# Two fused transformer blocks: the front and the indexer in another order, modulations moved into the gates, merging products moved into the last attention head

## The chip, the core and the metric

The kernel runs on one core of a Trainium2 chip. The metric is the device time of one execution in microseconds (us). Five engines work side by side, each through its own queue of instructions: PE (TensorE, matmuls; PEld are its weight loads), DVE (VectorE), ACT (ScalarE), POOL (GpSimd) and SP (SyncE, which here only starts transfers). They wait for each other through semaphores. Transfers between the main memory and the on-chip memory are done by 16 DMA engines, and are started here from the queues of SP, POOL and ACT. PSUM is the memory with eight banks into which PE writes.

## The reference

The input x has 1024 tokens of 1024 features. A first block and then two layers of a second block are applied to it. The change lies in the first block:

```python
h = rms_norm(x, g_mix)
aq, ak, av, bq, bk, bv, iq, ik, iw, cx, cy, gt = split_cols(h @ w_in)
y_a = chunk_relpos_attention(...)                       # 4 heads
q_i = apply_rope(iq, cos, sin); k_i = apply_rope(rms_norm(ik, g_idx_k), cos, sin)
# indexer: 4 heads of 64; each query keeps the 256 keys with the largest score
dots  = einsum('bqhe,bse->bqhs', q_i, k_i)
score = einsum('bqhs,bqh->bqs', relu(dots), w_i)
y_b = attention over the kept keys                      # 4 heads
y_c = rglru_branch(cx, cy, ...)                         # a linear recurrence (LRU)
gates  = sigmoid(gt + b_gate)                           # 3 x 1024 features
merged = gates[0] * (y_a @ wb_a) + gates[1] * (y_b @ wb_b) + gates[2] * (y_c @ wb_c)
x = x + merged @ w_out                                  # then a feed-forward part
```

Each layer of the second block scales and shifts its normed input by numbers that come from a condition alone, `silu(cond) @ w_ada + b_ada` (1024 x 3072 weights for each of two layers). These products are called modulations here: they need nothing of the first block and can be computed at any time before it ends. Its differential attention needs a number lambda, `exp(sum) - exp(sum) + const`, and sinks, which also depend on weights alone.

## The kernel before

All large products keep about single precision with three passes: each operand is split into a high part (a cast to a shorter format) and a low part (the rest), and `matmul3` (L2939) sums high x high, high x low and low x high. A split therefore takes an ACT cast (L3137 for weights, L3141 for values, L3154 for normed rows) and a DVE subtraction (L3297, L3300, L3322).

`schedule()` writes one list of steps in program order; then one function per engine goes through the list and issues its engine's share. So the order in which `schedule()` adds steps is the order on every engine's queue, and a step that waits holds up all later steps of its engine. The stages up to the merge are, in the profile's time:

- 0 to 79 us, the front. `t_x` loads x in 16 tiles (8 row groups, 2 chunks of 512 tokens) from POOL's queue, and `t_c` the constants from SP's. `w_load` and `w_prep` load and split weights (`w_get(name, ahead)` hands one out and prepares the next). `first_sums(c)` squares a chunk (ACT L3145 squares one tile, DVE L3305 squares and adds), `first_norm` then needs column sums on PE (L2976), the root on ACT (L3150), its reciprocal (DVE L3308), a spread over rows (PE L2983) and the scaling of every tile (DVE L3317). `cond` is the silu of the condition (ACT L3190). The three projections of the indexer are `ik`, `q0`, `q1` (weights ikw, iq0, iq1).
- up to 146 us, the keys and the indexer. `begin` rotates q or k (PE L2990, DVE L3330, POOL L3720), `end` sums the rotation (DVE L3334) and splits it. The keys stand on partitions 0 to 63 and are copied to 64 to 127 by DMA, since the four heads of the indexer use the two halves. `lambda` is on DVE (L3346), ACT (L3178) and DVE (L3349 to L3352). `index` is PE's product of a block b of 128 queries with its keys, one for each of four heads (24 in all, counted by `nr`); ACT takes the relu (L3183), DVE weighs and adds it (L3361, L3364).
- 146 to 473 us, eight column blocks (cx, cy) of the recurrent branch and 24 gates (`gt`), each 16 steps of three matmuls; a gate's result is stored from ACT's queue (L3132). DVE finds the largest scores here. Then the LRU.
- the attention heads, and from 931 us the merge: for each of 8 output groups d and 2 chunks c three places, `wb_first` (place 0, four steps of the recurrent branch), then the other two branches; DVE multiplies each by its gate (L3484 and following). In the last head the attention leaves PE time, into which a `Fill` of other steps is drawn (`early_steps` and the tail `wb_early`).

A modulation is eight small matmuls (PE L3021, 2 columns by 512), with two weight loads of 512 KB from SP's queue through a ring of buffers (`m_fetch`, L3748); after every second one `modrows` copies a row (ACT L3188), and the next modulation first does a turning (`m_turn`, PE L3026). There are 24 of them.

## Time and profile before

| | |
|---|---|
| median of 3 runs | 3783.07 us (3779.55 to 3783.47) |
| profiled execution | 3786.55 us, of which the span of the trace 3784.4 us |
| mean granted clock of PE | 0.952 |
| PE busy | 91% of the span |
| DVE, ACT, POOL busy | 56%, 37%, 8% |
| bytes moved | 257.16 MB |

A line number is that of the kernel before. In a row of the timeline the first number is the start after the span's beginning and the second the time the group takes; in brackets stands how long the engine had been idle and what it waited for. `m` is a buffer in on-chip memory, `PS` one in PSUM, `in_...` an input in main memory. A row with "x7" is a run of seven instructions. In the table of stretches the granted clock is a share of full speed: 1.00 stands for 2.4 GHz and 0.50 for 1.2 GHz.

### The profile page before, as it was taken

The numbers are of one execution on the slowest core, as the hardware profiler recorded it, in microseconds if no ns is written. First come the engines' busy times: TensorE is split into PE (matmuls) and PEld (weight loads), VectorE is DVE, ScalarE is ACT, GpSimd is POOL, SyncE is SP. The second block draws the span as 40 slices with busy tenths as digits, with TensorE's granted clock in tenths as the row PEclk, the third lists the DMA queues.
The fourth block names the chain that finished last, engine by engine and source line by source line (L and its number), as shares of the span: only waits on it lengthen the run. The fifth ranks groups of instructions, "written<-read, shape, count | busy, mean of one in ns | idle before, by whom it ended". The sixth has DMA issues, their size and how long they took to land. (4 is left out here: it accounts for less than half of the span.)

```text
span 3784.4 us, 43717 instructions
## 1 busy us (share of the span) xinstructions
PE 3455.7 (91%) x17694; PEld 2679.9 (71%) x17694; DVE 2124.7 (56%) x3918; ACT 1411.4 (37%) x2581; POOL 297.7 (8%) x431
## 2 busy tenths in 40 slices
PE   6999988897998999999899988888799999988888
PEld 4677766565877888887765677777677666676677
DVE  5799953444757666665556554455354444334444
ACT  3322264444233222322333244444324555434441
POOL 1122210001111000000000000000001000000000
PEclk9799999998999999999999998998799999989999
DMA  3333320002522222332210100010211101010112
GB/s 123 117 123 134 139 91 17 30 23 100 189 92 73 77 82 84 111 131 81 84 31 25 49 23 30 23 36 33 102 64 62 33 33 33 23 35 7 35 54 85
DMA packets 76632, 257.16 MB, mean 68 GB/s; under 512 B 9928, under 2 KB 11976, under 8 KB 76432
## 3 DMA queue, kind: packets, MB, share of 16 engines
q1 hardware_dynamic: 42192, 132.68, 10.5%
q0 software_dynamic: 30784, 109.12, 8.3%
q10 hardware_dynamic: 3456, 12.58, 0.8%
q8 instruction: 139, 2.28, 0.2%
q14 instruction: 61, 0.50, 0.0%
HBM read 193.53 MB, written 50.32 MB: 64 GB/s over the span
## 5 line engine op out<-in xcount | busy, mean ns | idle before, releaser
L2940 PE MATMUL PS<-m,m 128*128 128x512 f32 (+3 forms) x3476 | 1395.5, 403 | 84.2 <-DVE m L3297 16.8
L2942 PE MATMUL PS<-m,m 128*128 128x512 f32 (+3 forms) x3476 | 1338.3, 386 | 0.0
L2941 PE MATMUL PS<-m,m 128*128 128x512 f32 (+3 forms) x3476 | 1337.1, 386 | 0.0
L2940 PEld LDWEIGHTS PS<-m,m 128*128 128x128 f32 (+2 forms) x3476 | 664.3, 192 | 318.9 <-issue 77.0
L2942 PEld LDWEIGHTS PS<-m,m 128*128 128x128 f32 (+2 forms) x3476 | 664.1, 192 | 133.7 <-issue 0.8
L2941 PEld LDWEIGHTS PS<-m,m 128*128 128x128 f32 (+2 forms) x3476 | 667.7, 193 | 119.7 <-issue 1.5
L3229 ACT COPY m<-PS 128x512 f32<-128x512 f32 x352 | 205.1, 588 | 455.2 <-PE PS L3056 454.6
L3066 PE MATMUL PS<-m,m 128*64 128x256 f32 (+1 forms) x1408 | 307.8, 410 | 28.7 <-ACT m L3229 21.6
L3300 DVE TENSOR_TENSOR m<-m,m 128x512 fp32r<-128x512 f32 (+3 forms) x303 | 233.6, 790 | 163.0 <-ACT m L3141 161.9
L3141 ACT CAST m<-m 128x512 fp32r<-128x512 f32 (+3 forms) x303 | 198.7, 690 | 327.7 <-DVE m L3514 182.8
L3047 PE MATMUL PS<-m,m 64*128 64x256 f32 (+5 forms) x1968 | 248.0, 362 | 45.3 <-ACT m L3218 25.7
L3047 PEld LDWEIGHTS PS<-m,m 64*128 64x128 f32 (+1 forms) x1968 | 209.4, 193 | 93.8 <-ACT m L3218 33.6
L3056 PE MATMUL PS<-m,m 128*128 128x128 f32 x1408 | 227.7, 286 | 49.2 <-DVE m L3589 21.1
L3297 DVE TENSOR_TENSOR m<-m,m 128x1024 fp32r<-128x1024 f32 (+4 forms) x156 | 160.9, 1031 | 167.7 <-ACT m L3137 166.8
L3056 PEld LDWEIGHTS PS<-m,m 128*128 128x128 f32 x1408 | 169.7, 145 | 118.5 <-issue 39.8
L3161 ACT COPY m<-PS 128x512 f32<-128x512 f32 (+2 forms) x187 | 101.7, 549 | 331.9 <-PE PS L2942 331.8
L3066 PEld LDWEIGHTS PS<-m,m 128*64 128x64 f32 (+1 forms) x1408 | 155.0, 167 | 83.9 <-ACT m L3229 40.2
L3137 ACT CAST m<-m 128x1024 fp32r<-128x1024 f32 (+4 forms) x187 | 168.0, 900 | 120.0 <-PE PS L2942 58.0
L3520 DVE TENSOR_REDUCE m<-PS 128x1 f32<-128x1024 f32 x96 | 114.3, 1219 | 150.9 <-PE PS L3047 150.8
L3541 DVE CUSTOM_DVE_ANT_0 m<-PS,m 128x640 f32<-128x640 f32 (+7 forms) x128 | 93.1, 727 | 183.8 <-PE PS L3047 99.7
L3218 ACT ACTIVATE m<-PS,m 128x256 f32<-128x256 f32 (+1 forms) x272 | 188.1, 704 | 14.6 <-DVE m L3525 14.6
L3495 DVE TENSOR_TENSOR m<-m,PS 128x512 f32<-128x512 f32 x180 | 123.2, 685 | 116.5 <-PE PS L2942 113.6
(204 smaller groups left out, 3198.8 us busy)
## 6 DMA issues: line engine op xcount, KB each, us to landing
m<-in_w SPq DMA_DIRECT2D x222, 512.0 KB, 3.8
g_scratch<-m ACTq DMA_DIRECT2D x24, 512.0 KB, 2.6
m<-g_scratch POOLq DMA_DIRECT2D x24, 512.0 KB, 4.8
u_scratch<-m POOLq DMA_DIRECT2D x40, 256.0 KB, 3.2
m<-u_scratch POOLq DMA_DIRECT2D x20, 512.0 KB, 4.2
m<-in_w SPq DMA_DIRECT2D x40, 256.0 KB, 4.0
x_scratch<-m POOLq DMA_DIRECT2D x2, 4096.0 KB, 13.4
m<-m POOLq DMA_DIRECT2D x60, 128.0 KB, 2.7
```

Source lines behind the costliest of these rows:

```text
L2940: pe.e.engine.matmul(o, L[0], X[0], start=start, stop=False)
L2941: pe.e.engine.matmul(o, L[0], X[1], start=False, stop=False)
L2942: return pe.e.engine.matmul(o, L[1], X[0], start=False, stop=stop)
L3047: m = e.matmul(o, L, X, start=first, stop=last)
L3056: m = e.transpose(PS[:, s["out"] + 128 * i:s["out"] + 128 * i + 128], x, ident)
L3066: m = e.matmul(O, L, X, start=start, stop=stop)
L3137: e.copy(s["hi"], s["src"]).then_inc(*act.says(S.hi, ("w", s["i"])))
L3141: e.copy(s["hi"], s["src"]).then_inc(*act.says(S.hi, n))
L3218: m = e.activation(d, src if bias is None else d, ACT.Exp, bias=sums[:, 0:1], scale=scale, accum_out=sums[:, 3 + a:4 + a])
L3229: e.copy(s["h"], s["src"]).then_inc(*act.says(S.hi, ("pt", s["u"], s["g"])))
L3297: e.tensor_tensor(s["lo"], s["src"], s["hi"].bitcast(F), ALU.subtract).then_inc(*dve.says(S.lo, ("w", s["i"])))
L3300: e.tensor_tensor(s["lo"], s["src"], s["hi"].bitcast(F), ALU.subtract).then_inc(*dve.says(S.lo, n))
```

## The change

The first half's squares come before the weights' casts; the cast of the third weight and the silu come after the first norm; four of the x tiles are loaded from ACT's queue. The keys are summed, split and copied by chunks, and q0's and q1's second halves and lambda come between the indexer's blocks. The first three modulations leave the front, two leave the indexer, and every gate up to the last modulation runs one. In the last head the merging product of (output group 0, chunk 0) moves from the tail into the fill, and that of (1, 0) enters the tail.

```diff
@@ -1254,3 +1254,4 @@
     t_c = [move(vec[:, :], vec_d[:, 0:NVEC]), move(cst[:, :], cst_d)]
-    t_x = {(k, t0): move(X[:, k, t0:t0 + tn], xT[k][:, t0:t0 + tn]) for t0, tn in CH1 for k in range(8)}
+    t_x = {(k, t0): move(X[:, k, t0:t0 + tn], xT[k][:, t0:t0 + tn], on="pool" if t0 or k % 2 else "act")
+           for t0, tn in CH1 for k in range(8)}
     t_blam = move(blam[:, :], vec_d[:, NVEC:NVEC + 256])
@@ -1320,10 +1321,10 @@
 
+    early_sums = first_sums(0)
     w_prep(2)
-    p.add("cond", csil=csil[:, :], cond=vc("cond", 0, 16))
-    first = first_norm(0, first_sums(0))
+    first = first_norm(0, early_sums)
     next(first)
     w_load(3)
-    w_prep(3)
-    m_fetch(RING, [t_x[7, 0]])
     finish(first)
+    w_prep(3)
+    p.add("cond", csil=csil[:, :], cond=vc("cond", 0, 16))
 
@@ -1357,5 +1358,3 @@
             second = first_norm(1, late_sums)
-            steps_of(ik, 6)
-            modulate()
-            steps_of(ik, 2)
+            steps_of(ik, 8)
             steps_of(q0, 8)
@@ -1439,14 +1438,14 @@
             finish(q1)
-            modulate()
-            p.add("lambda", blam=[blam[:, 64 * i:64 * i + 64] for i in range(4)], ld=ld[:, :], lam=lam_t, after=t_blam,
-                  sink=vc("sink", 0, 8), nsink=nsink[:, :])
-            k_t = end("k", 0) + end("k", 1)
-            d1 = move(ikh[64:128, :], ikh[0:64, :], k_t)
-            d2 = move(ikl[64:128, :], ikl[0:64, :], k_t)
+            key_t = []
+
+            def keys_down(c):
+                t0, tn = CH1[c]
+                t = end("k", c)
+                key_t.append([move(x[64:128, t0:t0 + tn], x[0:64, t0:t0 + tn], t) for x in (ikh, ikl)])
+
+            keys_down(0)
             begin("q1", 1)
-            end("q0", 1)
-            modulate(last=True)
-            end("q1", 1)
+            keys_down(1)
             ring, m_rows = late_ring, late_rows
-            m_fetch(2 * m_next[0] + RING, normed + [(S.mod, m_all[m_next[0] - 1])])
+            m_fetch(RING, normed)
             b = take()
@@ -1456,3 +1455,2 @@
             bank_free[b] = [(S.score, "wi")]
-            p.add("ready", on="pe", after=qk_t + [d1, d2])
             r_free = [[], []]
@@ -1462,2 +1460,10 @@
                 sc = score[b]
+                if b in (2, 4):
+                    p.add("ready", on="pe", after=qk_t + key_t[b // 2 - 1])
+                if b == 2:
+                    end("q0", 1)
+                    p.add("lambda", blam=[blam[:, 64 * i:64 * i + 64] for i in range(4)], ld=ld[:, :], lam=lam_t, after=t_blam)
+                if b == 3:
+                    end("q1", 1)
+                    p.add("lambdas", lam=lam_t, sink=vc("sink", 0, 8), nsink=nsink[:, :])
                 for h in range(4):
@@ -1478,3 +1484,3 @@
                     nr += 1
-                    if nr % 4 == 0:
+                    if nr >= 12 and nr % 4 == 0:
                         modulate(nr == 24, [(S.lru, "lambda")])
@@ -1547,3 +1553,3 @@
                 for n, _ in enumerate(linear_steps(f"gt{i}_{d}", h_rhs, CH1, ev_s)):
-                    if n == 7 and n_g % 2 == 0 and m_next[0] < len(m_all):
+                    if n == 7 and m_next[0] < len(m_all):
                         modulate()
@@ -1626,7 +1632,8 @@
 
-            def wb_early():
-                y_held["w"] = w_get("wb0")
-                for c in range(2):
-                    b = y_held[c] = (7, 0)[c]
-                    yield from wb_first(0, c, b, y_held["w"])
+            def wb_early(jobs):
+                for d, c, b in jobs:
+                    if c == 0:
+                        y_held[d] = w_get(f"wb{d}", 2 - d)
+                    y_held[d, c] = b
+                    yield from wb_first(d, c, b, y_held[d])
             for kind in "ab":
@@ -1666,2 +1673,3 @@
                         yield from early_steps(list(ready) + list(second))
+                        yield from wb_early([(0, 0, 7)])
                     for k_, j_ in nxt:
@@ -1715,4 +1723,4 @@
                 more = (8 if nxt and nxt[0][0] == "b" else 6) + 32 if nxt else 0
-                at.run(units, ready, Fill(steps(), more + (18 if n_ab else 0) + (0 if nxt else 14)), 18 if n_ab else 0, tail,
-                       None if nxt else Fill(wb_early(), 8))
+                at.run(units, ready, Fill(steps(), more + (18 if n_ab else 0) + (0 if nxt else 18)), 18 if n_ab else 0, tail,
+                       None if nxt else Fill(wb_early([(0, 1, 0), (1, 0, 2)]), 8))
                 if nxt:
@@ -1737,10 +1745,10 @@
             y_ready[k] = split(Yh[:, k, :], Yl[:, k, :], y_in[:, k, 0:T], [y_there[k]])
-        p.turns += (1 - p.turns) % 6
+        p.turns += (4 - p.turns) % 6
         for d in range(8):
-            get, kt, release, event = weights = y_held["w"] if d == 0 else w_get(f"wb{d}")
+            get, kt, release, event = weights = y_held[d] if d in y_held else w_get(f"wb{d}")
             for c, (t0, tn) in enumerate(CH1):
                 for place, (i, k0, k1) in enumerate(((2, 4, 8), (0, 0, 2), (1, 2, 4))):
-                    b = y_held[c] if d == 0 and place == 0 else take()
+                    b = y_held[d, c] if place == 0 and (d, c) in y_held else take()
                     key = (f"wb{d}", c, i)
-                    if d and place == 0:
+                    if place == 0 and (d, c) not in y_held:
                         finish(wb_first(d, c, b, weights))
@@ -1762,2 +1770,4 @@
             release((S.lin, key))
+            if d == 0:
+                w_prep(st["use"] + 1)
         p.fence(False)
@@ -3347,2 +3357,4 @@
                                        lam[:, 2 + i:3 + i]).then_inc(*dve.says(S.lru, ("lambda", i)))
+        elif s.kind == "lambdas":
+            lam = s["lam"]
             dve.wait_ge(S.lruact, "lambda")
```

ACT's queue at the start of the program, before (m_67 is x, m_51 and m_52 raw weights, m_57 the vectors):

```order
L3137 ACT_TABLE_LOAD
L3137 CAST m_53<-m_51 128x544
L3137 CAST m_54<-m_52 128x1024
L3190 ACT_TABLE_LOAD
L3190 ACTIVATE m_65<-m_57 128x16
L3145 ACTIVATE m_70<-m_67 128x512
```

The squares (L3145, in the changed kernel L3155) are now the first work of the queue, behind four tile loads; the casts of the two weights follow them.

ACT's queue after the change, from the last scaled tiles of the first norm to the first squares of the second half (m_82 is the third weight's high part, m_65 the silu):

```order
L3164 CAST m_49<-m_71 128x512
L3164 CAST m_49<-m_72 128x512
L3147 CAST m_82<-m_51 128x1024
L3200 ACT_TABLE_LOAD
L3200 ACTIVATE m_65<-m_57 128x16
L3155 ACTIVATE m_76<-m_67 128x512
L3155 ACTIVATE m_74<-m_67 128x512
L3155 ACTIVATE m_75<-m_67 128x512
```

Before, the squares (L3145) stood directly behind the scaled tiles (L3154), and the cast of m_82 before them.

DVE's queue at the keys, before (m_97 is the keys, m_103 their low part, m_60 holds lambda):

```order
L3330 TENSOR_TENSOR m_105<-PS,m_59 128x512
L3346 ISA m_80,m_60<-m_81 128x64
L3346 ISA m_60 128x1
L3346 ISA m_80,m_60<-m_81 128x64
L3346 ISA m_60 128x1
L3349 TENSOR_TENSOR m_60<-m_60 128x1
L3351 TENSOR_SCALAR m_60<-m_60 128x1
L3352 TENSOR_SCALAR m_60<-m_57 128x8
L3334 TENSOR_TENSOR m_97<-m_108,m_109 64x512
L3300 TENSOR_TENSOR m_103<-m_97,m_102 64x512
```

The same queue after the change (m_95 is q0, m_114 the head weights wi):

```order
L3340 TENSOR_TENSOR m_105<-PS,m_59 128x512
L3344 TENSOR_TENSOR m_97<-m_108,m_109 64x512
L3310 TENSOR_TENSOR m_103<-m_97,m_102 64x512
L3340 TENSOR_TENSOR m_107<-PS,m_59 128x512
L3344 TENSOR_TENSOR m_97<-m_110,m_111 64x512
L3310 TENSOR_TENSOR m_103<-m_97,m_102 64x512
L3367 TENSOR_SCALAR m_114<-PS 128x32
L3344 TENSOR_TENSOR m_95<-m_104,m_105 128x512
L3310 TENSOR_TENSOR m_100<-m_95,m_98 128x512
L3356 ISA m_80,m_60<-m_81 128x64
```

The key sums have moved ahead of lambda, and lambda behind q0's second half.

PE's queue in the last head before, from the last products of attention with values to the last scores (m_49 and m_50 are the halves of two of the recurrent branch's groups, m_53 and m_55 those of the weight):

```order
L3066 MATMUL PS<-m_186,m_156 64x256 x2
L3047 MATMUL PS<-m_154,m_152 128x512 x2
L3047 MATMUL PS<-m_155,m_152 128x512 x2
L3047 MATMUL PS<-m_154,m_153 128x512 x2
L3047 MATMUL PS<-m_154,m_152 128x512 x2
L3047 MATMUL PS<-m_155,m_152 128x512 x2
L3047 MATMUL PS<-m_154,m_153 128x512 x2
L2940 MATMUL PS<-m_49,m_53 128x512
L2941 MATMUL PS<-m_50,m_53 128x512
L2942 MATMUL PS<-m_49,m_55 128x512
```

After the change, behind the last scores (m_190 and m_191, m_150 and m_151 are two more groups of the recurrent branch):

```order
L3057 MATMUL PS<-m_154,m_153 128x512 x2
L2950 MATMUL PS<-m_49,m_53 128x512
L2951 MATMUL PS<-m_50,m_53 128x512
L2952 MATMUL PS<-m_49,m_55 128x512
L2950 MATMUL PS<-m_190,m_53 128x512
L2951 MATMUL PS<-m_191,m_53 128x512
L2952 MATMUL PS<-m_190,m_55 128x512
L2950 MATMUL PS<-m_150,m_53 128x512
L2951 MATMUL PS<-m_151,m_53 128x512
L2952 MATMUL PS<-m_150,m_55 128x512
L2950 MATMUL PS<-m_49,m_53 128x512
L2951 MATMUL PS<-m_50,m_53 128x512
```

Where one step of a merging product stood behind the scores, four stand now: three of the moved product (its first stands ahead of the scores) and the first of the tail.

## Rows read from the trace of the kernel before

**Rows 1.** busy time by engine and its share of the span, from the page
```profile
PE 3455.7 (91%) x17694; PEld 2679.9 (71%) x17694; DVE 2124.7 (56%) x3918; ACT 1411.4 (37%) x2581; POOL 297.7 (8%) x431
```

**Rows 2.** five stretches: us, busy time by engine, granted clock, DMA share
```profile
core 0: us, PE busy (x) PEld busy (x) DVE busy (x) ACT busy (x) POOL busy (x), PEclk, DMA share, GB/s
2.00:9.00 7.00, 0.00 (x0) 0.00 (x0) 0.28 (x1) 0.46 (x1) 6.55 (x13) 1.00 0.96 326
79.00:86.00 7.00, 6.94 (x10) 2.75 (x11) 3.30 (x6) 0.00 (x0) 3.74 (x3) 0.51 0.01 2
93.00:137.00 44.00, 35.10 (x153) 23.01 (x155) 18.74 (x30) 14.26 (x23) 2.39 (x3) 0.50 0.42 130
146.00:473.00 327.00, 327.00 (x1513) 260.00 (x1512) 325.88 (x609) 69.41 (x91) 66.19 (x32) 1.00 0.34 127
931.00:1024.00 93.00, 92.82 (x393) 74.42 (x393) 75.97 (x106) 18.32 (x26) 9.04 (x18) 0.98 0.45 157
```

**Rows 3.** timeline of the front, all engines: start, length, what ended the wait
```profile
8.54 1.28 ACT L3137 ACT_TABLE_LOAD   x1 [8.54 <-DMA m<-in_cst]
...
9.84 1.59 ACT L3137 CAST m<-m 128x544 fp32r<-128x544 f32 x2
...
12.74 0.21 ACT L3190 ACTIVATE m<-m 128x16 f32<-128x16 f32 x1
...
21.68 1.03 ACT L3137 CAST m<-m 128x1024 fp32r<-128x1024 f32 x1
...
33.28 0.62 ACT L3154 CAST m<-m 128x512 fp32r<-128x512 f32 x1 [0.64 <-DVE m L3317]
...
34.98 5.47 DVE L3305 TENSOR_TENSOR m<-m,m 128x512 f32<-128x512 f32 x7 [0.36 <-ACT m L3145]
...
41.34 0.95 PE L2976 MATMUL PS<-m,m 128*128 128x1 f32 x8
```

**Rows 4.** timeline from 76 to 110 us, the keys
```profile
79.06 5.63 PE L2990 MATMUL PS<-m,m 64*64 64x512 f32 x6 [2.62 <-DVE m L3312]
...
88.16 0.58 ACT L3161 COPY m<-PS 128x512 f32<-128x512 f32 x1 [10.52 <-PE PS L2942]
...
91.62 0.68 DVE L3334 TENSOR_TENSOR m<-m,m 64x512 f32<-64x512 f32 x1
...
96.22 1.10 POOL L3708 DMA_DIRECT2D m<-m  x2 [10.17 <-DVE m L3300]
...
104.73 0.69 PE L2940 MATMUL PS<-m,m 64*128 64x384 f32 x2 [7.90 <-DMA m<-m]
```

**Rows 5.** DMA issues from 84 to 150 us: KB each, us to landing
```profile
m<-m POOLq DMA_DIRECT2D x2, 256.0 KB, 7.6
```

**Rows 6.** DMA issues of the whole span, from the page
```profile
m<-in_w SPq DMA_DIRECT2D x222, 512.0 KB, 3.8
...
m<-m POOLq DMA_DIRECT2D x60, 128.0 KB, 2.7
```

**Rows 7.** timeline of PE in the indexer, up to cx0
```profile
113.58 1.87 PE L3026 MATMUL PS<-m,m 128*128 128x2 f32 x8
115.38 1.89 PE L3021 MATMUL PS<-m,m 128*2 128x512 f32 x8
...
124.20 0.79 PE L2940 MATMUL PS<-m,m 64*128 64x512 f32 x1
...
145.66 0.50 PE L2940 MATMUL PS<-m,m 128*128 128x512 f32 x1
```

**Rows 8.** timeline of ACT in the gates, the stores alone
```profile
263.16 0.33 ACTq L3132 DMA_DIRECT2D g_scratch<-m  x1
...
276.05 0.33 ACTq L3132 DMA_DIRECT2D g_scratch<-m  x1
...
286.93 0.33 ACTq L3132 DMA_DIRECT2D g_scratch<-m  x1
...
299.00 0.33 ACTq L3132 DMA_DIRECT2D g_scratch<-m  x1
```

**Rows 9.** timeline of DVE, the first LRU step
```profile
489.27 1.23 DVE L3434 TENSOR_TENSOR m<-m,m 128x1024 f32<-128x1024 f32 x1 [12.65 <-ACT m L3203]
```

More of the change, by code:

```diff
@@ L1319, in first_sums @@
         return sums
+    early_sums = first_sums(0)
     w_prep(2)
-    p.add("cond", csil=csil[:, :], cond=vc("cond", 0, 16))
-    first = first_norm(0, first_sums(0))
+    first = first_norm(0, early_sums)
     next(first)
     w_load(3)
+    finish(first)
     w_prep(3)
-    m_fetch(RING, [t_x[7, 0]])
-    finish(first)
+    p.add("cond", csil=csil[:, :], cond=vc("cond", 0, 16))
     with mem:
```

## The prediction

> **What bounds the kernel now.** The first view to read is the busy time by engine [rows 1]: PE (TensorE) is busy 91% of the span, so a change that shortens the kernel must take work or waiting out of PE. The second is the table by stretch [rows 2], which says where there is something to take: from 146 to 473 us (the column blocks of the recurrent branch and the gates) PE is busy all 327.00 us at a granted clock of 1.00, so there every instruction more is paid in full; from 93 to 137 us (end of the front, the indexer) it is busy only 35.10 of 44 us, at a clock of 0.50, that is at 1.2 GHz instead of 2.4; from 931 to 1024 us (the merge) it is again full, 92.82 of 93 us. The third view is the timeline of the places that the change edits: the front [rows 3], the keys [rows 4, 5, 6], the indexer [rows 7], the gates [rows 8] and the first LRU step [rows 9]. The reader is to see in rows 4 that the indexer's first product starts at 104.73 after 7.90 us of waiting for a copy by DMA, and that behind the wait stands a chain: the lambda exponential, the key sum on DVE at 91.62, the POOL issues at 96.22, and the landing 7.6 us later [rows 5].
>
> **Front.** In what follows f is how much later the second half's norm ends. On ACT the two casts (1.59), the table load (1.28, the length of the one at 8.54) and the silu (0.21) leave the place ahead of the first squares [rows 3]: 3.08 us in all, less the 0.1 by which such instructions overlap, 3.0, and that is what the first half gains, g, if the constants still land at 8.54. They may not: the DMA engines are 0.96 busy at 326 GB/s from 2 to 9 us [rows 2], and four x tiles of 256 KB now set out on ACT's queue instead of behind the others on POOL's; 1.05 MB at 326 GB/s is 3.2 us, so the constants land 0 to 3.2 us later. I take the middle, g = 1.45, since no row shows which queue goes first. In the second half the cost turns round. Before, the late squares followed the last norm cast (33.28 + 0.62) at once; now the cast of the third weight (1.03, which stood at 21.68), a table load (1.28) and the silu (0.21) lie between: 2.5 us on the path, as DVE's additions wait for ACT's squares there. The additions end at 34.98 + 5.47 = 40.45 before; now at 34.98 + 2.5 + 0.1 − g + 5.47, some 43.0 − g. PE's column sums stood at 41.34, held by PE's own products in front of them; those now end at 41.3 − g, so PE waits 1.7 to 1.95 us and f = 1.7 − g = +0.25 (−1.3 to +1.7). A wait of that size also touches the clock: the 2.62 us of idleness at 79.06 [rows 4] was followed by 7 us at 0.51 [rows 2], which costs 7 × 0.49 = 3.4. Whether this shorter wait does the same no row says; between 0 and 3.4 I take 1.7. So f = 1.9 us in the forecast, −1.3 to +5.1 at the ends.
>
> The four moved tiles meet a rule of the Trainium skill, in "DMA: Bandwidth & Descriptors", section "Issuing engines are not separate DMA queues": transfers started by different engines run on the same 16 DMA engines and interleave, so spreading them saves only the starting time. The share of 0.96 agrees that there was nothing idle to spread them over. By the rule the constants lose the full 3.2 us; I give that a chance of its own below.
>
> The new table load meets another, in "ScalarE: Activation LUTs", section "What ACT_TABLE_LOAD costs": a drain of about 1.38 us goes with each switch of sets. The trace disagrees: the casts end at 11.43, the silu starts at 12.74, 1.31 us for a load of 1.28 [rows 3]. By the page f would be 1.4 us larger; the sum goes by the rows.
>
> **Keys.** Lambda leaves the chain of the keys, which are copied by chunk. ACT's copy at 88.16 ends at 88.74; before, ACT then did the modulation's copy, a table load and the exponential, and DVE three small steps, until the key sum at 91.62. Now the first chunk's cast follows the copy (0.62, as the one at 33.28), its lower part on DVE 0.69: 90.05 + f. The two issues on POOL, 0.55 us each, and 2.7 us for a copy of 128 KB [rows 6] give 93.4 + f; by the slower copies of this stretch, 7.6 us, 98.3 + f. What is late next is DVE and ACT: behind the keys DVE has wi, q0's sum and split, the four lambda products, then the relu additions of block b=2, q1's sum and split and the lambda steps, then block b=3. ACT's first relu stands behind the lambda exponential, about 96.3 + f. Adding the durations of such steps (an estimate from 0.68 each, as at 91.62) DVE is through with b=3 at about 102.0 + f, and PE, two banks ahead, ends b=4 at 106.6 + f. One modulation at half clock, 1.89 [rows 7], and b=5 starts at 108.5 + f, where it started at 124.20 before. From there to cx0, at 145.66, the old indexer took 21.46 us; one turning of the two in it (1.87 at half clock) goes, so 19.4 or so remain if the clock comes back after as much work as before (the stretch at 0.50 ended at 137). cx0 starts at about 127.9 + f: the keys and the indexer gain 17.8 us before f. If the half clock stays to the end of the indexer, the 8.66 us that ran at full clock from 137 on, less a turning of 0.8, take up to 7.8 more; I put 6.3, as not all in them is matmul: gain 11.5. If the full clock returns already in b=5, the 12.8 us from 124.20 to 137, less the turning's 1.87, shrink by up to a half: 10.9 × 0.48 = 5.2, gain 23.0.
>
> **Gates.** The modulations are not gone. Before cx0 there were 9 and 4 turnings, now 4 and 1; the cx and cy blocks keep their 4; the gates had 11 and have 16, so that 3 turnings more come after cx0. The stores of the gates give the price at full clock [rows 8]: 286.93 − 276.05 = 10.88 for a gate with nothing in it, 299.00 − 286.93 = 12.07 with a modulation, 276.05 − 263.16 = 12.89 with a turning too: 1.19 and 0.82. That is 5 × 1.19 + 3 × 0.82 = 8.4 us, on a PE that has no idle time to put them in. The LRU that follows does not take this back: DVE waits there for ACT's gates 12.65 us [rows 9], and those wait for PE.
>
> **Merge.** Twelve matmuls of the first place, chunk (1,0), leave the merge for the last head: 92.82 / 393 = 0.236 each, 2.8 us, and as PE is full in the merge that is earned if the last head doesn't end later. It does a little: two more casts of 128x512 (0.62 each) stand before exponentials in its third unit, and the cast of wb1 (1.03) in its last; I put 1.1 and 0.4 on the path, 0.2 less if idle ACT time takes some, 3.3 at most if DVE's lower parts come after. Net 1.3, from −0.5 to 2.8. Moving (0,0) from the tail to the fill, and (1,0) to the tail, exchanges equal work in PE's waiting time.
>
> **Sum.** 17.8 − 1.9 − 8.4 + 1.3 = 8.8 us. The profiled execution took 3786.55 us, so 3777.75 for such a one; the median of the runs, 3783.07, lies 3.48 lower, which gives 3774.3 us.
>
> **Rivals.** *The constants land 3.2 us late.* For it: the engines' share of 0.96. Then g is 0, f = 1.7 + 1.7 = 3.4, and the sum 7.3: 3775.8. Against it: before, 13 POOL issues already fell into these 7 us [rows 2], and the constants still landed by 8.54.
>
> *The clock comes back early.* With the modulations at the head of the indexer gone, PE has fewer two-column products and more plain ones in that stretch; the gain there is 23.0, the sum 14.0: 3769.1. Against it: PE waits for DVE in b=2 and b=3 now, and after each wait of rows 4 the clock was low.
>
> *The clock stays low to cx0.* More short waits, in a stage that is shorter: the gain is 11.5, the sum 2.5, and the time 3780.6, which is within 0.2% of before. For it: the old stage needed from 93 to 137 us.
>
> *The weights come late in the gates (slower).* SP's queue issues a gate's weights behind the two 512 KB loads of a modulation, and these wait until an earlier modulation has freed its buffer. Now that stands in 16 gates in a row instead of 11 alternating ones. The slack is about 10 us (half a gate, and one whole of 10.88, less some 6 for cast and subtract). If the three loads run one after the other at 3.8 us each [rows 6] they take 11.4, PE waits 1.4 in each of 16 gates, 22.4 in all, and the kernel is 13.6 slower: 3796.7. It decides as soon as three loads need over 10 us. Against it: the DMA share from 146 to 473 us is 0.34, so that they should overlap, and the 11 gates that had this order already show no wait in 327.00 us.
>
> **How the numbers follow.** Forecast 0.38, constants late 0.10, clock early 0.17, clock low 0.27, weights late 0.08. The forecast alone would reach from 3769 (f = −1.3, all of the merge) to 3780 (f at its upper end, the copy of 7.6 us). For 8 in 10 I add the early clock and the low one with its own bad ends: 3764 to 3786. A measurement of this kernel can tell about 0.2%, 7.6 us, from no change: faster means below 3775.5. The forecast lies there with 0.6, the late constants with 0.4, the early clock always but for a hundredth, the low clock with 0.1: 0.47 in all. Slower (over 3790.6) is the last rival, 0.08; the rest, 0.45, is within 0.2%.
>
> **What would show it.** The first square starts at about 11.4; the second half's column sums stand behind a PE wait of nearly 2 us near 41.6, and the granted clock after it is low or not. The first index product starts near 95, cx0 near 129.8. The gate stores are 12.1 to 12.9 us apart for 16 gates in a row. The last head ends 1 to 2 us later against the front's shift, and the merge is 2.8 shorter. It is wrong if the first index product is still later than 100, if PE shows waits for weights between cx0 and the LRU, or if the clock in the indexer is not near 0.5.

## The result: 0.29% slower, lost mainly in the one place that was called equal work

The changed kernel takes 3792.79 us (median of 7 runs, 3790.05 to 3796.97), the kernel before 3782.55 in the same comparison: a ratio of 1.0029, with a 95% interval of 1.0020 to 1.0039. The forecast was 3774.3, within 3764 to 3786: wrong in sign and outside the range.

The first view to read after such a result is not the page (PE is busy 91% as before, at a clock of 0.953 against 0.952) but the start of the same instruction in both traces, stage by stage. Subtracting them shows where the time goes. Each line gives one instruction, and how much later (+) or earlier (−) it starts in the changed kernel:

| instruction | us |
|---|---|
| spread of the second half's norm (PE) | +1.3 |
| first relu of the indexer (ACT) | −9.2 |
| first matmul of cx0 (PE) | −16.2 |
| first LRU gate product used (DVE) | −7.4 |
| end of the LRU (DVE) | −8.2 |
| first scores of the first head (DVE) | −6.2 |
| first multiply of the merge (DVE) | −6.0 |
| third multiply of the first place in the merge (DVE) | −1.8 |
| fifth one (DVE) | +3.1 |
| column sums of the next norm (PE) | +5.6 |
| column sums at 1,662 us (PE) | +7.2 |
| column sums at 2,318 us, in the second block (PE) | +10.6 |
| a copy in the last attention (ACT) | +7.0 |

Up to the LRU the sum is as forecast (−7.5 was forecast there). Then, from the merge's first multiply to the next norm, PE loses 11.5, of which 9.1 up to the fifth multiply. Another 3.4 go in the second block.

The stretches of the changed kernel (columns as in [rows 2]):

```profile
core 0: us, PE busy (x) PEld busy (x) DVE busy (x) ACT busy (x) POOL busy (x), PEclk, DMA share, GB/s
2.00:9.00 7.00, 0.00 (x0) 0.00 (x0) 0.00 (x0) 0.00 (x0) 6.32 (x12) 1.00 1.00 361
42.00:46.00 4.00, 4.00 (x11) 3.17 (x12) 0.18 (x1) 0.54 (x2) 0.00 (x0) 0.57 0.02 4
93.00:128.00 35.00, 31.69 (x151) 23.29 (x152) 21.93 (x40) 19.11 (x28) 1.60 (x3) 0.61 0.33 102
146.00:473.00 327.00, 326.94 (x1542) 254.96 (x1541) 316.89 (x563) 74.70 (x96) 64.35 (x27) 1.00 0.38 139
931.00:951.00 20.00, 12.23 (x30) 9.12 (x31) 9.88 (x14) 2.18 (x3) 0.00 (x0) 0.66 0.09 29
951.00:1024.00 73.00, 73.00 (x317) 59.08 (x316) 58.66 (x84) 13.78 (x19) 8.46 (x16) 1.00 0.47 159
```

The fifth line is new: from 931 to 951 us, where PE was full before [rows 2], it is busy 12.23 of 20 us, at a clock of 0.66. The waits of PE between 915 and 960 us say for whom (total, times, longest):

```profile
PE PS L2950 <- DVE m L3496: 8.9, 2, 5.0
PE PS L2950 <- DVE m L3310: 3.0, 2, 2.8
```

And the timeline shows what stands on either side of the two waits (all engines; start, length, wait):

```profile
933.06 0.69 DVE L3496 TENSOR_TENSOR m<-PS,m 128x512 f32<-128x512 f32 x1
933.80 0.80 PE L2950 MATMUL PS<-m,m 128*128 128x512 f32 x1 [3.90 <-DVE m L3496]
...
943.52 0.68 DVE L3496 TENSOR_TENSOR m<-PS,m 128x512 f32<-128x512 f32 x1
...
944.26 0.80 PE L2950 MATMUL PS<-m,m 128*128 128x512 f32 x1 [4.96 <-DVE m L3496]
```

L3496 (L3484 before) is DVE's multiply of a sum's first place; it reads the PSUM bank in which that place was summed and so frees it. PE's matmul that waits for it is the second place of the same sum. Why it waits is in the code: the change counts the banks of the merge from 4, so the second and third places take, for (group 0, chunk 0), banks 4 and 5; for (0, 1), banks 0 and 1; for (1, 0), banks 2 and 3. But bank 0 holds the first place of (0, 1), and bank 2 that of (1, 0), both finished ahead in the last head's tail. PE's second place must not overwrite the first before DVE has multiplied it, and DVE does that only after it has finished the sum before. So PE stops behind DVE at each of the two.

The same count does it a third time. It is not set anew after the merge, so a merge that starts at another bank shifts the banks of later products too. In the second block the first product after an attention then takes bank 5, which the attention's output still holds (its output banks are 4 and 5); before, it took bank 3. PE waits for ACT's copy out of it (first the changed kernel, then the kernel before, same matmul and the 7 us from there):

```profile
2159.31 0.79 PE L2950 MATMUL PS<-m,m 128*128 128x512 f32 x1 [4.99 <-ACT m L3274]
```

```profile
2159.00:2166.00 7.00, 6.69 (x17) 5.27 (x18) 3.04 (x5) 0.57 (x2) 0.55 (x1) 0.56 0.22 92
```

```profile
2150.27 0.40 PE L2940 MATMUL PS<-m,m 128*128 128x512 f32 x1
```

```profile
2150.00:2157.00 7.00, 7.00 (x33) 5.78 (x32) 5.74 (x6) 0.96 (x3) 0.00 (x0) 1.00 0.00 0
```

This wait stands in the four profiles in which the count starts at 4 or 3, and in no other. The wait and the low clock behind it cost 6.5 us in the changed kernel; some 3 are gained shortly before, from 1,850 to 1,950 us. From 1,850 to 2,210 us these four lose 3.4 to 7.3 us net, the others at most 1.2.

### The profile page after: what moved, and what is told of

It reads as the page before. It is cut to its first block and busy times, and to the rows that moved or that the text cites. A ratio compares the mean times of both kernels' runs of the same rounds, so it can differ in the third digit from the quotient of the medians.

```text
span 3791.2 us, 43724 instructions
## 1 busy us (share of the span) xinstructions
PE 3456.8 (91%) x17694; PEld 2679.5 (71%) x17694; DVE 2126.0 (56%) x3918; ACT 1413.4 (37%) x2582; POOL 296.6 (8%) x429
```

## The experiments

Line numbers in a row are those of the kernel it is from. The kernels were timed in three comparisons, on three chips, each with the kernel before beside it: its medians are 3780.83 for the first four (merging part taken back, merging part alone, other banks, weights as early as before), 3780.76 for the next four and 3781.57 for the last four. Kernels of different comparisons are set against each other by their differences to it; the changed kernel stands 10.2 above it.

**The merging part taken back.** The tail, the fill and the banks as before, all else as changed:

```diff
...
-            def wb_early(jobs):
+            def wb_early():
...
-                        yield from wb_early([(0, 0, 7)])
...
-                       None if nxt else Fill(wb_early([(0, 1, 0), (1, 0, 2)]), 8))
+                       None if nxt else Fill(wb_early(), 8))
...
-        p.turns += (4 - p.turns) % 6
+        p.turns += (1 - p.turns) % 6
...
-            if d == 0:
-                w_prep(st["use"] + 1)
...
```

> The changed kernel with the merging part taken back: the tail holds the two products of output group 0 in banks 7 and 0, as before. Theory A (banks: in the changed kernel two later products are written into the bank that still holds their own sum's first product, so PE waits for DVE's multiply, 3.9 and 5.0 us, and then runs at half clock): these go, and the rest of the change stands, 3776 us, 6 us below before. Theory B (weights: the third output group's weights are prepared too late): the same here. If neither is the cause and the loss is in the front or the attention: no better than 3788.

Measured: 3775.80 us, ratio 0.9987 (0.9979 to 0.9996), 5.0 below the kernel before and so 15.3 below the changed kernel. The rest of the change does gain, though 5.0 and not the 7.5 that the forecast has without the merge; the merging part costs all of it and more. This fits both theories.

**The merging part alone**, in the kernel before: the lines of the diff above, from before to after.

```diff
...
-        p.turns += (1 - p.turns) % 6
+        p.turns += (4 - p.turns) % 6
...
+            if d == 0:
+                w_prep(st["use"] + 1)
...
```

> The kernel before with the merging part alone. Theories A and B: 9 to 13 us slower than before, 3792 to 3796, with two waits of PE for the merge's multiply near 940 and 950 us. If the loss comes of the earlier start of the whole first part (other clock, other meeting of transfers): within 3 us of before.

Measured: 3802.08 us, ratio 1.0050 (1.0036 to 1.0064), 21 slower and above what either theory gave. In its trace the two waits are there, 8.8 us together, and from the merge's first multiply to the next norm 11.7 are lost, as 11.5 are in the changed kernel. Another 7.3 net arise between 1,850 and 2,210 us: 3.7 with the third wait, as above, and 3.6 behind it, where the clock is at 0.50 from 2,200 to 2,204 us and at 1.00 in the changed kernel, with no wait in the rows to account for it. The merging part is shown as the place of the loss; its price in the merge is about 12 us, and what it costs behind differs between profiles.

**Other banks.** The order and the weights of the changed kernel, with banks that nobody holds:

```diff
-        p.turns += (4 - p.turns) % 6
+        p.turns += -p.turns % 6
+        own = {(0, 0, 1): 4, (0, 0, 2): 5, (0, 1, 1): 3, (0, 1, 2): 1, (1, 0, 1): 4, (1, 0, 2): 5}
...
-                    b = y_held[d, c] if place == 0 and (d, c) in y_held else take()
+                    b = y_held[d, c] if place == 0 and (d, c) in y_held else own.get((d, c, place))
+                    b = take() if b is None else b
```

> The changed kernel with other banks for the six later products of the three sums that are begun early, so that none is written into a bank that holds a first product not yet multiplied; order and weights as in the changed kernel. Theory A: both waits go, PE is full from the merge's start, 11 to 14 us less than the changed kernel: 3774 to 3780, below before by some 5 to 8. Theory B: no change, 3790 to 3794.

Measured: 3777.29 us, ratio 0.9986 (0.9978 to 0.9995): 3.5 below the kernel before, so other bank numbers are worth 13.8 us. The waits of PE from 905 to 960 us, and the stretch that was at 0.66:

```profile
PE PS L2952 <- DVE m L3312: 2.9, 2, 2.8
PE PS L2952 <- DVE m L3498: 0.5, 1, 0.5
```

```profile
931.00:951.00 20.00, 19.55 (x85) 15.51 (x84) 16.71 (x24) 3.76 (x5) 1.58 (x3) 1.00 0.32 115
```

The first wait stood in the changed kernel too; of the 8.9 us for the multiply (here L3498) 0.5 are left, and the clock is full. Theory A holds, B falls. The edit moves the later count as well, and the third wait is gone with the two. The two profiles divide the gain: 13.0 us between the merge's first multiply and the next norm, 3.6 in the second block.

**A smaller dose.** Counting from 3 moves the collision from the second place to the third, six matmuls later:

```diff
-        p.turns += (4 - p.turns) % 6
+        p.turns += (3 - p.turns) % 6
```

> The changed kernel with the banks of the merge counted from 3 instead of 4: now it is the last of the three places, six matmuls or 1.4 us later, that is written into the bank of the sum's own first product. If a wait for DVE's multiply through the bank is the cause, its price falls by about 1.4 us each and the half clock behind it shortens: waits of some 2.5 and 3.6 us instead of 3.9 and 5.0, 3783 to 3789 against 3792.8 of the changed kernel. If any wait at all is enough for the whole loss (a clock that falls in any case): 3790 or more. If the banks were not the cause: 3790 to 3795, with the same waits.

Measured: 3784.50 us, ratio 1.0011 (1.0002 to 1.0020). PE's waits, in its timeline:

```profile
929.97 0.50 PE L2950 MATMUL PS<-m,m 128*128 128x512 f32 x1 [2.43 <-DVE m L3496]
...
936.60 0.79 PE L2950 MATMUL PS<-m,m 128*128 128x512 f32 x1 [3.56 <-DVE m L3496]
```

2.43 and 3.56 us stood in the expectation as 2.5 and 3.6. With 8.9, 6.0 and 0.5 us of such waits, the stretch from the merge's first multiply to the next norm takes 11.5 and 5.1 longer than before, and 1.5 less. The loss follows the wait, and is 1.2 to 2.2 us for each us of it (6.6 for 5.5, 6.5 for 2.9). What comes on top is the clock behind the wait: in the changed kernel PE's matmuls start 0.43 us apart there, and 0.23 when the clock is back.

```profile
937.38 0.63 PE L2952 MATMUL PS<-m,m 128*128 128x512 f32 x1
937.81 0.63 PE L2950 MATMUL PS<-m,m 128*128 128x512 f32 x1
...
951.37 0.39 PE L2951 MATMUL PS<-m,m 128*128 128x512 f32 x1
951.60 0.40 PE L2952 MATMUL PS<-m,m 128*128 128x512 f32 x1
```

From 905 to 1,030 us 37 matmuls start that far apart in the changed kernel and 17 with the other banks. Twenty times 0.2 is 4.1 us, and with 8.4 us more of waiting this gives 12.5 of the 13.0.

**The weights as early as before.** This leaves out the order that keeps the split of the third group's weights off buffers from which group 0 still reads; the instructions are the same in number and kind.

```diff
-                        y_held[d] = w_get(f"wb{d}", 2 - d)
+                        y_held[d] = w_get(f"wb{d}")
...
-            if d == 0:
-                w_prep(st["use"] + 1)
```

> The changed kernel with the weights prepared as far ahead as before: the third output group's weights are cast and subtracted when the second's are fetched, in the tail of the last head, instead of after group 0. Theory A: no change, 3790 to 3795 (the cast of 1.04 and the subtraction of 1.22 us in the tail could even cost 1). Theory B: at least 5 us less than the changed kernel.

Measured: 3790.24 us, ratio 1.0024 (1.0015 to 1.0033): 9.4 above the kernel before, only 0.8 less than the changed kernel. Theory B is out as the cause. The second wait is shorter, 3.68 us instead of 4.96:

```profile
943.60 0.62 PE L2948 MATMUL PS<-m,m 128*128 128x512 f32 x1 [3.68 <-DVE m L3494]
```

In the changed kernel the subtraction of the third group's weights (1.22 us on DVE, at 942.38) stands just ahead of the multiply for which PE waits; so the late weights lengthen the loss by about 1.3 us without being its cause.

**The late squares without work ahead of them.** From here on the merging part is the old one. The third weight's cast goes behind the second half's squares, the silu behind that norm:

```diff
-    w_prep(3)
-    p.add("cond", csil=csil[:, :], cond=vc("cond", 0, 16))
...
             late_sums = first_sums(1)
+            w_prep(3)
...
             finish(second)
+            p.add("cond", csil=csil[:, :], cond=vc("cond", 0, 16))
...
```

> The changed kernel without the merging part, and with the third weight's cast behind the second half's squares and the silu behind the second norm, so that no cast, table load or silu stands ahead of those squares. Theory of the prediction (2.5 us on ACT's path to the column sums make PE wait 1.9 us and fall to half clock for 4 us): the wait goes, and 2 to 4 us: 3772 to 3774 against 3775.8. Rival (the copy of the keys sets the indexer's start in any case): no change, 3774.5 to 3777.

Measured: 3773.60 us, ratio 0.9984 (0.9976 to 0.9993), and 3773.98, ratio 0.9984 (0.9975 to 0.9993), when it was run again as "late_again", whose expectation was the same time:

> The same kernel as in the comparison before (the changed one without the merging part and with the mended front), on the same chip and beside the three above, for their differences: 3773.6, with 1.5 us either way.

PE's column sums then follow its own matmuls with no wait, 2.2 us earlier than in the changed kernel:

```profile
38.71 0.95 PE L2982 MATMUL PS<-m,m 128*128 128x1 f32 x8
```

The gain, 2.1 and 2.6 us against the kernel with the merging part taken back, has the direction and size of the theory, not far above the medians' scatter. That the clock has a part in it is not shown: in the profile of that kernel the wait is there, 1.94 us, but the clock behind it is at 1.00 (the rows stand under "Front" below). Against that profile the column sums and the spread both stand 2.4 us earlier, so that behind the wait nothing more is gained.

**The old front.** Casts and silu ahead of the first squares, x from POOL's queue alone; merging part old.

```diff
-    t_x = {(k, t0): move(X[:, k, t0:t0 + tn], xT[k][:, t0:t0 + tn], on="pool" if t0 or k % 2 else "act")
+    t_x = {(k, t0): move(X[:, k, t0:t0 + tn], xT[k][:, t0:t0 + tn])
...
-    early_sums = first_sums(0)
...
-    first = first_norm(0, early_sums)
+    p.add("cond", csil=csil[:, :], cond=vc("cond", 0, 16))
+    first = first_norm(0, first_sums(0))
...
+    w_prep(3)
...
-    w_prep(3)
-    p.add("cond", csil=csil[:, :], cond=vc("cond", 0, 16))
...
```

> The changed kernel without the merging part and with the old front (casts and silu ahead of the first squares, x from POOL's queue alone). The prediction's front term (1.9 us later): 3774. Rival (the front gains what the first squares gain, 2 us, since the indexer follows the first half): 3778. The clock in the indexer may come early or late by chance and spread single runs by 8 us; the medians should tell.

Measured: 3778.39 us, ratio 0.9995 (0.9986 to 1.0003): 2.7 slower than with the new front, so the new front is no loss and probably a gain. Its own trace doesn't show why: the second half's spread stands 0.6 earlier than with the new front, yet the first index product 4.0 later (92.55 against 88.57) and cx0 5.2 later. The clock differs between the two profiles in that stretch, and it differs between profiles of the same instructions as well. It stays open.

**Two modulations back in the indexer.**

```diff
-                    if nr >= 12 and nr % 4 == 0:
+                    if nr % 4 == 0:
```

> The changed kernel without the merging part, with two of the modulations moved back into the indexer, behind its blocks 2 and 3. By the prediction's rates: 2 x 1.89 and up to 2 x 1.87 us at half clock come in, 2 x 1.19 and 0.82 at full clock leave the gates, 2 to 4 us slower: 3778 to 3780. Rival (PE waits in blocks 2 and 3 for DVE and ACT anyway, and the modulations fill that time and keep the clock up): the 3.2 us of the gates are gained: 3772 to 3773.

Measured: 3782.50 us, ratio 1.0003 (0.9994 to 1.0012), 6.8 slower, beyond the 2 to 4 that were expected. In the profiles the way from the first index product to cx0 takes 42.9 us instead of 33.1, and the gates give back 3.2 less; together that is 6.6 slower. A part of it is a wait of 1.12 us for the second one's weights:

```profile
97.01 1.89 PE L3027 MATMUL PS<-m,m 128*2 128x512 f32 x8
...
103.93 1.89 PE L3027 MATMUL PS<-m,m 128*2 128x512 f32 x8 [1.12 <-DMA m<-in_w]
```

Moving these modulations into the gates, where each costs 1.19 us, is therefore right.

**Whole keys.** With the mended front, the keys copied by two transfers of 256 KB after both chunks:

```diff
-                t = end("k", c)
-                key_t.append([move(x[64:128, t0:t0 + tn], x[0:64, t0:t0 + tn], t) for x in (ikh, ikl)])
+                key_t.append(end("k", c))
+                if c:
+                    key_t[:] = [[move(x[64:128, :], x[0:64, :], key_t[0] + key_t[1]) for x in (ikh, ikl)]] * 2
```

> The changed kernel without the merging part, with the mended front, and with the keys copied whole, 256 KB twice, when both chunks are split; lambda stays behind them. The first index product waits for both: issue near 94 instead of 91 us, and 256 KB that took 7.6 us instead of 128 KB in 2.7: up to 8 us later. If the chunks matter: 4 to 9 us slower, 3778 to 3783. If DVE's work in blocks 2 and 3 sets the pace anyway: 3774 to 3776.

Measured: 3777.76 us, ratio 0.9990 (0.9981 to 0.9999), 3.8 slower than with chunks. The first index product waits longer, 7.61 us, and starts at 92.83 instead of 89.86:

```profile
92.83 0.69 PE L2947 MATMUL PS<-m,m 64*128 64x384 f32 x2 [7.61 <-DMA m<-m]
```

The copy of 256 KB took 3.3 us here, not the 7.6 of before [rows 5], so its length there was not the size's doing alone:

```profile
m<-m POOLq DMA_DIRECT2D x2, 256.0 KB, 3.3
```

Of the 3.0 us at the first product 1.6 are left at cx0. The rest of the 3.8 arises from cx0 to the LRU, where both kernels have the same steps (11.1 us are given back instead of 8.4); no row ties that to the keys.

**All x tiles from POOL's queue.** Merging part old, front mended.

```diff
-    t_x = {(k, t0): move(X[:, k, t0:t0 + tn], xT[k][:, t0:t0 + tn], on="pool" if t0 or k % 2 else "act")
+    t_x = {(k, t0): move(X[:, k, t0:t0 + tn], xT[k][:, t0:t0 + tn])
```

> The changed kernel without the merging part, with the mended front, and with all x tiles loaded from POOL's queue as before. By the measured landing of the constants (9.52 us against 8.54) the first squares could start 1.0 us earlier, 3772.6 against 3773.6. Rival (from one queue the later tiles of the first half come too late for the squares, and these wait): 0 to 2 us slower, 3773.6 to 3776.

Measured: 3775.94 us, ratio 0.9986 (0.9977 to 0.9995), against 3773.98. Its constants land about 1.2 us earlier, but the first squares start only 0.41 earlier, at 10.23 instead of 10.64, since they now wait for an x tile, as the rival has it:

```profile
8.94 1.28 ACT L3151 ACT_TABLE_LOAD   x1 [8.94 <-DMA m<-in_xT]
```

The column sums stand 0.4 earlier; yet the median is 2 higher. The two don't fit, and I put the median down to neither side.

**Both mends.** The banks that don't collide, and the late squares first.

> The changed kernel with the merging part in banks that don't collide, and the front's casts and silu behind the second half's squares: the two mends together. Theory of the prediction (twelve matmuls, 2.8 us, leave a merge in which PE is full, and 1.5 of it is lost in the last head): 1 to 2.5 us below the kernel that has the old merging part and the same front, that is 3771 to 3773. Rival (the time that PE gains in the merge is given back at the next norm, where it waits for DVE and the clock falls): no gain, 3773 to 3776.

Measured: 3773.22 us, ratio 0.9979 (0.9970 to 0.9988): the fastest version, 8.4 below the kernel before, but only 0.8 below the one with the old merging part, which is no difference that these runs can tell. It lies within the rival's range and 0.2 above the theory's; the medians can't decide between the two. In its trace the merge's first multiply stands 13.0 earlier than before, and the next norm's column sums 14.4 earlier: 1.5 us are gained in the merge. Of these 1.3 go at that norm (13.1 earlier behind it). PE waits there equally long for DVE in this kernel and in the one with the old merging part, but the clock behind the wait differs. The waits, and then the 7 us behind them, first in this kernel:

```profile
PE PS L2988 <- DVE m L3317: 2.9, 1, 2.9
```

```profile
PE PS L2982 <- DVE m L3311: 2.9, 1, 2.9
```

```profile
1097.00:1104.00 7.00, 6.80 (x22) 5.74 (x23) 0.33 (x2) 0.26 (x1) 0.00 (x0) 0.54 0.46 151
```

```profile
1098.00:1105.00 7.00, 6.79 (x31) 5.77 (x32) 0.69 (x3) 0.26 (x1) 0.00 (x0) 0.76 0.44 151
```

At 0.54 against 0.76 PE does 22 matmuls instead of 31. Five of the six profiles with the merging part lose 1.3 to 1.6 us at this norm, the changed kernel too, which reaches it 5.6 later than before, and none of those without. So it is not the earlier arrival that takes the gain; what does stays open.

## Why the prediction was wrong, step by step

**Front: right on ACT's path, the clock by chance.** The constants landed at 9.52, 1.0 us late (1.45 was put), so the squares gained 2.0. The column sums waited as forecast (1.94 us; 1.7 to 1.95 was put) and stood 0.4 earlier than before, and the spread came 1.3 later; 1.9 was put. The lines that answer to [rows 3]:

```profile
9.52 1.28 ACT L3155 ACT_TABLE_LOAD   x1 [9.52 <-DMA m<-in_cst]
...
10.82 1.67 ACT L3155 ACTIVATE m<-m 128x512 f32<-128x512 f32 x3
...
32.83 1.28 ACT L3200 ACT_TABLE_LOAD   x1
...
34.13 0.22 ACT L3200 ACTIVATE m<-m 128x16 f32<-128x16 f32 x1
...
40.95 1.05 PE L2986 MATMUL PS<-m,m 128*128 128x1 f32 x8 [1.94 <-DVE m L3315]
```

The price of the clock was put at 1.7, in the middle between nothing and 3.4, and from the column sums to the spread 5.34 us passed instead of 3.68, which is 1.7 more: there the clock was 0.57, in the table above. That is luck. With the merging part taken back the same wait stands in the trace, and the clock is full behind it:

```profile
41.15 1.05 PE L2982 MATMUL PS<-m,m 128*128 128x1 f32 x8 [1.94 <-DVE m L3311]
```

```profile
42.00:46.00 4.00, 4.00 (x23) 3.47 (x24) 0.18 (x1) 0.75 (x2) 0.00 (x0) 1.00 0.02 4
```

In the six profiles with this front the spread stands from 0.6 earlier to 2.2 later than before.

One sentence ahead of the prediction is wrong: the constants are loaded from POOL's queue, ahead of the x tiles, not from SP's. The Trainium skill ("DMA: Bandwidth & Descriptors", section "Issuing engines are not separate DMA queues") says that transfers started by different engines run on the same 16 DMA engines and interleave. The trace agrees in kind: with four tiles from ACT's queue the engines went from 0.96 to 1.00 busy, and the constants issued beside them came 1.0 us later. That they would lose the full 3.2 us, as the prediction reads the rule, doesn't follow from interleaving and was not seen. The Trainium skill ("ScalarE: Activation LUTs", section "What ACT_TABLE_LOAD costs") puts a drain of about 1.38 us with each switch of sets. The trace disagrees in the changed kernel too: 32.83 to 34.13 is 1.30 us for a load of 1.28.

**Keys and indexer: right in the path, near in the number partly by luck.** First product at 94.29 (95.3 was put), cx0 at 129.45 (129.8):

```profile
91.09 1.10 POOL L3720 DMA_DIRECT2D m<-m  x2 [3.92 <-DVE m L3310]
...
94.29 0.70 PE L2950 MATMUL PS<-m,m 64*128 64x384 f32 x2 [2.96 <-DMA m<-m]
...
96.82 0.85 ACT L3193 ACTIVATE m<-PS 128x384 f32<-128x384 f32 x2
```

With the merging part taken back, whose instructions are the same up to there, cx0 starts 7.8 us earlier still. Of these 1.5 arise from 42 to 46 us, some 4 between 60 and 89 us, and only 2.1 from the first index product to cx0. So the forecast's bounds for the clock were real, but the clock varied in the front as much as in the indexer. The stretch from 93 us in that profile (it holds later work than in the table above, as all stands 5.7 or more earlier):

```profile
93.00:128.00 35.00, 33.61 (x175) 24.25 (x173) 24.88 (x54) 18.74 (x26) 0.78 (x5) 0.78 0.41 144
```

**Gates: right.** From cx0 to the LRU 8.8 us are given back (8.4 was put); the stores stand 12.08 and 12.88 apart, and PE shows no wait for weights in 326.94 of 327 us, so the slower rival of the prediction did not happen.

```profile
249.34 0.33 ACTq L3142 DMA_DIRECT2D g_scratch<-m  x1
...
262.22 0.33 ACTq L3142 DMA_DIRECT2D g_scratch<-m  x1
...
274.30 0.33 ACTq L3142 DMA_DIRECT2D g_scratch<-m  x1
```

**Not in the sum: the first head.** Between the LRU's end and the first scores 2.0 us go. PE waits longer there for a weight's lower part (first the changed kernel, then before):

```profile
551.36 0.79 PE L2950 MATMUL PS<-m,m 128*128 128x512 f32 x1 [5.76 <-DVE m L3307]
```

```profile
559.55 0.50 PE L2940 MATMUL PS<-m,m 128*128 128x512 f32 x1 [4.14 <-DVE m L3297]
```

The wait itself ends 8.2 earlier, as the LRU does; what is lost stands behind it, where the same 48 matmuls take 13.6 us instead of 12.4 to the last one's start. It is not the steps alone: with the other banks, whose order there is the same, the stretch takes 50.3 us as before, against 52.2 in the changed kernel.

**Merge: wrong, and the step that failed.** "Moving (0,0) from the tail to the fill, and (1,0) to the tail, exchanges equal work in PE's waiting time" counted matmuls and not the banks they are summed into. The merging part was put at 1.3 us gained, and the place of the banks in it at nothing. In its place the runs show 8.9 us of waits for PE and a clock of 0.66 around them: the changed kernel lost 11.5 us in the merge, and 3.4 in the second block, where the same count brings the third wait. By the medians the merging part costs 15.3. The result lies 19.0 us above the forecast (10.2 slower instead of 8.8 faster): 16.6 of these are the merging part, and the rest is that everything else gave 5.0 instead of 7.5.

The two sizes in this term were off as well, and cancel, which is luck. With banks that don't collide the merge gains 1.5 and not 2.8, and the last head costs 0.1 to 0.5 and not 1.5; the net is about 1.2, and the next norm takes as much.

The clue stood in the diff: `p.turns += (4 - p.turns) % 6` next to a tail that holds banks 0 and 2. Writing down the six bank numbers would have shown the collision; PE being full in that stretch [rows 2] then says that the wait is paid in full. No rival had this mechanism: the chance of 0.08 for slower stood for a late weight load, in another stage. That no other stage would be touched went unsaid in the prediction, and the third wait shows that it is not so.

## What to carry to other kernels

When a product is begun early and kept in PSUM, list which bank each later product takes until the kept one is read: a round-robin that starts in the wrong place makes the tensor engine wait for the reader's whole queue. Where the count runs on, follow it to the end of the program. Price a new wait of a full tensor engine at more than its length (here 1.2 to 2.2 times), because the clock can fall behind it. And look for the loss by subtracting the starts of the same instruction in two traces: busy shares of both kernels were the same to a tenth of a per cent here.

## What the runs showed of the hardware that was not expected

The granted clock in one stage is not fixed by the instructions, nor by the wait ahead of it. In the front the same wait of 1.94 us was followed by 0.57 in one profile and by 1.00 in another. Far behind all edits the same 176 matmuls ran at 0.96 in the changed kernel and at 0.83 with the weights as early as before:

```profile
2637.00:2677.00 40.00, 26.45 (x176) 22.66 (x176) 26.04 (x47) 23.43 (x52) 2.12 (x4) 0.96 0.19 66
```

```profile
2634.00:2674.00 40.00, 30.49 (x176) 26.30 (x176) 24.81 (x47) 20.46 (x44) 2.11 (x4) 0.83 0.18 66
```

Between the norms on either side of this stretch the changed kernel gains 3.6 us on the other, which had led it by 3.1. Single executions of one kernel spread by 6 to 15 us for this reason or another that no run tells apart, so effects of 2 us need many runs, and some above stay open.
